# A hybrid decoder block on one core: k, the recurrent gate and both merge gates as seven products of half blocks

## What is computed

```
h = rms_norm(x, norm_mix_g)
proj = h @ w_in                      # 1024 x 7168: xr, gr, q, k, v, g0, g1, 1024 columns each
gates = sigmoid(g0, g1)
y_rnn = rglru_branch(xr, gr, ...)    # conv, gates r and i, linear recurrence, times gelu(gr)
y_att = diff_attention(q, k, v, ...) # 8 heads
merged = gates[0] * (y_rnn @ w_proj_rnn) + gates[1] * (y_att @ w_proj_att)
x = x + merged @ w_out
x = x + moe_ffn(rms_norm(x, norm_ffn_g), ...)   # top 4 of 32 experts
return rms_norm(x, norm_final_g)
```

## Time and profile before

| | |
|---|---|
| median of 3 executions | 1226.13 us (1225.16 to 1226.57) |
| profiled execution | 1225.36 us, of which the span from first to last instruction is 1223.6 |
| TensorE busy | 1165.2 us, 95% |
| VectorE, ScalarE, GpSimd busy | 294.6, 177.3 and 41.3 us |
| mean granted TensorE clock | 0.992 |
| transfers | 452.86 MB, mean 370 GB/s |

### The profile page before, as it was taken

How to read it: one execution, slowest core, us unless ns; L and a number is a source line. 1 busy time by engine, 2 the same in 40 slices (tenths; PEclk the granted TensorE clock), 3 DMA queues, 4 the chain that set the end, 5 groups by cost and what they waited for, 6 DMA issues and landing times.

```text
span 1223.6 us, 13719 instructions
## 1 busy us (share of the span) xinstructions
PE 1165.2 (95%) x5598; PEld 581.3 (48%) x5598; DVE 294.6 (24%) x611; ACT 177.3 (14%) x354; POOL 41.3 (3%) x35
## 2 busy tenths in 40 slices
PE   9999999999999999999999989898998989898997
PEld 7588888885533434333343424333333333342432
DVE  2915656222322120211212120202021111111112
ACT  2123433102310101101010101000010101010102
POOL 1000005600000000000000000000000000000000
PEclk9999999999999999999999999999999999999999
DMA  9555534775999999999999999999999999999996
GB/s 289 183 181 206 206 138 147 282 292 223 370 399 426 428 432 428 435 425 435 427 435 425 435 427 437 424 436 426 437 428 433 430 432 428 432 430 428 433 423 273
DMA packets 51114, 452.86 MB, mean 370 GB/s; under 512 B 7412, under 2 KB 8558, under 8 KB 32142
## 3 DMA queue, kind: packets, MB, share of 16 engines
q1 hardware_dynamic: 51086, 452.47, 89.3%
HBM read 450.35 MB, written 1.06 MB: 369 GB/s over the span
## 4 chain that ended last, share of the span: by engine, by line
PE 66%; DMA 31%; DVE 1%; SPq 1%; issue 0%; ACT 0%; DVEq 0%; ACTq 0%
PE bank L1648 25%; PE bank L1385 17%; DMA arena<-in_w_up_e 16%; PE banks L1648 9%; DMA arena<-in_w_gate_e 7%; DMA w_gate_sb<-in_w_gate_e 5%; PE banks L1597 3%; DMA w_down_sb<-in_w_down_e 3%; PE bank L1545 2%; PE bank L1402 1%; PE banks L1419 1%; PE bank L1419 1%; PE bank L1691 1%; PE banks L1787 1%; PE banks L1843 1%; PE bank L1843 1%
## 5 line engine op out<-in xcount | busy, mean ns | idle before, releaser
L1648 PE MATMUL bank<-arena 128*64 128x512 f32 x1032 | 238.7, 607 | 21.6 <-DMA arena<-in_w_gate_e 13.6
L1385 PE MATMUL bank<-arena,w_down_sb 128*128 128x256 f32 x960 | 210.0, 380 | 0.0
L1385 PEld LDWEIGHTS bank<-arena,w_down_sb 128*128 128x128 f32 x960 | 181.3, 190 | 26.8 <-issue 1.5
L1648 PEld LDWEIGHTS bank<-arena 128*64 128x64 f32 x1032 | 72.6, 139 | 162.5 <-issue 146.6
L1648 PE MATMUL bank<-w_gate_sb,arena 128*64 128x512 f32 x508 | 117.6, 610 | 9.7 <-DMA w_gate_sb<-in_w_gate_e 9.7
L1648 PE MATMUL bank<-w_up_sb,arena 128*64 128x512 f32 x508 | 112.4, 594 | 13.8 <-DMA w_up_sb<-in_w_up_e 13.8
L1648 PE MATMUL bank<-w_down_sb,arena 128*64 128x512 f32 x480 | 105.5, 592 | 0.0
L1260 DVE TENSOR_SCALAR arena<-bank 128x512 f32<-128x512 f32 x32 | 22.1, 692 | 256.5 <-PE bank L1648 255.2
L1648 PEld LDWEIGHTS bank<-w_up_sb,arena 128*64 128x64 f32 x508 | 35.5, 137 | 85.5 <-issue 64.9
L1648 PEld LDWEIGHTS bank<-w_gate_sb,arena 128*64 128x64 f32 x508 | 35.4, 140 | 81.3 <-issue 67.3
L1172 DVE TENSOR_TENSOR arena<-banks,g2T 128x512 f32<-128x512 f32 (+1 forms) x32 | 21.9, 684 | 200.5 <-PE banks L1597 199.7
(11 more groups left out here) (318 smaller groups left out, 832.4 us busy)
## 6 DMA issues: line engine op xcount, KB each, us to landing
w_down_sb<-in_w_down_e SPq DMA_DIRECT2D x30, 2048.0 KB, 34.5
arena<-in_w_up_e SPq DMA_DIRECT2D x13, 4096.0 KB, 39.5
w_up_sb<-in_w_up_e SPq DMA_DIRECT2D x13, 4096.0 KB, 37.6
arena<-in_w_gate_e SPq DMA_DIRECT2D x13, 4096.0 KB, 30.8
w_gate_sb<-in_w_gate_e SPq DMA_DIRECT2D x12, 4096.0 KB, 30.1
arena<-in_w_down_e SPq DMA_DIRECT2D x14, 2048.0 KB, 29.3
w_gate_sb<-in_w_down_e SPq DMA_DIRECT2D x14, 2048.0 KB, 29.3
w_down_sb<-in_w_in SPq DMA_DIRECT2D x12, 2048.0 KB, 8.2
```

The lines of the kernel that those rows point to most:

```text
L1385: ins = eng.matmul(ps[:, n * T:(n + 1) * T], w[:, k, (2 * b + n) * P:(2 * b + n + 1) * P], rhs[:, k, :], start=(k == 0), stop=(k == KC - 1))
L1648: ins = eng.matmul(ps[b * JB:(b + 1) * JB, :], lhsT, w[:, h * CH:(h + 1) * CH], **flags)
```

## The change

k, gr, g0 and g1 are no longer in the list of chunks. Each is made by seven block products (28 units in place of 16). The weights of one of them are loaded as four blocks of 512 x 512 (1 MB, `block_load`); VectorE makes two sums of weights (`block_sum_one`, `block_sum_two`), GpSimd two more from the second (128x2048 elements each); `block_product` is 16 matmuls with a 128x128 block of weights or sums as the loaded operand and 128 tokens or token sums moving, and takes the token sums that v made. ScalarE takes out the first product and the upper left quarter (products 0 and 2, which add up in one bank), VectorE adds the five other parts from PSUM (128x512 each) to what lies in SBUF (`block_part`). The tanh of the three other quarters of g0 and g1 follows in `block_tanh`. The heads' loop has 11 steps with two of these units each (one in the last). Exp and Tanh of the recurrence move in front of q's outputs, all eight scans in front of the heads' loop, between the parts of k; the sums of gr's weights too. The first two gelu instructions of VectorE move from step 5 to step 6. Four semaphores of loads and that of GpSimd's memset are used again.

```diff
+        WQ = [WG[:, 2 * n:2 * n + 2, :]... for n in range(4)]
+        DQ = [wst[:, n // 2, n % 2 * KQ:(n % 2 + 1) * KQ, :] for n in range(4)]
+        EQ = tile(8, KQ)
+        blocks_at = [(WQ[0], WQ[1], WQ[2], DQ[0]), (WQ[0], WQ[3], DQ[3], DQ[2]),
+                     (WQ[0], DQ[1], WQ[1], DQ[0]), (WQ[0], WQ[3], DQ[2], UQ)]
+        sums_at = [(WQ[1], EQ, UQ, DQ[1]), (WQ[3], WQ[2], EQ, UQ), (DQ[1], DQ[3], WQ[2], EQ), (WQ[3], WQ[1], DQ[3], WQ[2])]
+        block_tile = [kT, xrT, iT, rT]
...
 # SyncE
+            eng.wait_ge(s["unit_done"], unit("v", 7) + 1)
+            block_load(0, 0)
+            block_load(0, 1)
+            chunk(5)
+            block_load(0, 2)
+            block_load(1, 1)
...
+            eng.wait_ge(s["unit_done"], unit("q", 1) + 1)
+            block_load(0, 3)
+            eng.wait_ge(s["unit_done"], unit("q", 3) + 1)
+            block_load(1, 3)
+            block_load(1, 2)
+            eng.wait_ge(s["unit_done"], block_done(0, 0))
+            eng.wait_ge(s["job_tiles_then_sums_ready"], block_pool_sums(0, 1))
+            block_load(1, 0)
...
 # GpSimd
+            for j in range(len(BLOCKED)):
+                eng.wait_ge(s["sums_ready"], block_sums(j, 2))
+                eng.wait_ge(block_loaded[0], 16 * (j + 2))
+                if j > 0:
+                    eng.wait_ge(s["unit_done"], block_done(j - 1, 1))
+                    eng.wait_ge(s["job_tiles_then_sums_ready"], block_pool_sums(j - 1, 2))
+                eng.tensor_tensor(three, two, b11, ALU.subtract).then_inc(s["job_tiles_then_sums_ready"], 1)
+                eng.wait_ge(block_loaded[2], 16 * (j + 2))
+                if j > 0:
+                    eng.wait_ge(s["unit_done"], block_done(j - 1, 3))
+                eng.tensor_tensor(four, b21, two, ALU.subtract).then_inc(s["job_tiles_then_sums_ready"], 1)
 # VectorE
+            def block_part(j, n):
+                eng.wait_ge(s["unit_done"], block_done(j, n))
...
+                eng.tensor_tensor(out, part, quarters(bank[unit(BLOCKED[j], n) % 2]), ALU.add).then_inc(s["parts_ready"], 1)
+            block_sum_one(0)
             eng.wait_ge(s["decay_ready"], 2 * KC)
             link(eng.tensor_scalar(xcT[:, :, :], yrT[:, :, :], 1.0, None, ALU.add))
-            link(eng.reciprocal(xcT[:, :, :], xcT[:, :, :]))
+            link(eng.reciprocal(xcT[:, 0:KQ, :], xcT[:, 0:KQ, :]))
+            block_sum_two(0)
+            link(eng.reciprocal(xcT[:, KQ:KC, :], xcT[:, KQ:KC, :]))
...
+            block_part(0, 1)
             eng.wait_ge(s["multiplier_ready"], 1)
             link(eng.tensor_tensor(iT[:, :, :], iT[:, :, :], rT[:, :, :], ALU.mult))
+            block_sum_one(1)
+            block_sum_two(1)
+            for n in range(3, 7):
+                block_part(0, n)
+                for c in (2 * n - 6, 2 * n - 5):
+                    ins = eng.tensor_tensor_scan(yrT[:, c, :], xrT[:, c, :], iT[:, c, :], 0.0, ALU.mult, ALU.add)
...
+            for step in range(11):
                 if 1 <= step <= H:
                     weights_in(step - 1)
+                for n in (2 * step, 2 * step + 1):
+                    if n < 21:
+                        block_part(1 + n // 7, n % 7)
                 if step < H:
                     scores_in(step)
+                if step in (0, 4):
+                    block_sum_one(2 if step == 0 else 3)
+                if step in (1, 5):
+                    block_sum_two(2 if step == 1 else 3)
 # TensorE
+            def block_product(j, n):
...
+                if n < 2:
+                    if j == 0:
+                        eng.wait_ge(s["unit_out"], u - 1)
+                    else:
+                        eng.wait_ge(s["parts_ready"], block_parts(j - 1, n + 4))
+                elif n in (2, 4):
+                    eng.wait_ge(s["unit_out"], block_out(j, n // 2))
+                else:
+                    eng.wait_ge(s["parts_ready"], block_parts(j, {3: 1, 5: 2, 6: 3}[n]))
...
+                if n in (1, 4):
+                    eng.wait_ge(s["sums_ready"], block_sums(j, 2))
+                if n in (3, 5):
+                    eng.wait_ge(s["job_tiles_then_sums_ready"], block_pool_sums(j, n // 2))
...
+                for f in range(KQ):
+                    for k in range(KQ):
+                        ins = eng.matmul(ps[:, f * P:(f + 1) * P], w[:, k, f * P:(f + 1) * P], tokens[:, k, :],
+                                         start=(n in (0, 1, 3, 4) and f == 0 and k == 0), stop=(k == KQ - 1),
+                                         skip_group_check=True)
```

More of the change, by code:

```diff
@@ L422, in apart @@
                 eng.dma_start(place, src[:, k, :]).then_inc(done, 16)
[L424 to L446, removed]
@@ new lines, in _ @@
+            swap_halves(6, 8, s["conv_swapped_high"])
+            eng.wait_ge(s["unit_done"], unit("v", 7) + 1)
[4 more added lines that the diff above has]
+            block_load(1, 1)
+            eng.wait_ge(s["bias_rows_cleared"], 1)
+            for copy in range(3):
+                rows = slice(copy * NE, (copy + 1) * NE)
+                for m, name in enumerate(["b_gate_e", "b_up_e", "b_down_e"]):
+                    eng.dma_start(brow[rows, m, :], A[name][0]).then_inc(s["late_tables_loaded"], 16)
@@ new lines, in _ @@
+            apart(3, "w_up_e", 1, s["first_steps_loaded"])
+            eng.wait_ge(s["unit_done"], block_done(3, 3))
+            chunk(7)
+            eng.wait_ge(s["unit_done"], block_done(3, 5))
+            steps("w_gate_e", 0, KQ, KC - 1, 0, half_loaded[0][1])
+            steps("w_down_e", 0, KC - 1, KC, 0, s["steps_ahead_loaded"])
+            eng.wait_ge(s["unit_done"], block_done(3, 6))
+            out_chunk(1)
+            for i in range(7, len(STREAM)):
+                if i > 7:
+                    chunk(i)
@@ L698, in _ @@
                                ).then_inc(s["decay_ready"], 1)
-            unit_out(unit("k"))
+            unit_out(unit("q"))
             eng.wait_ge(s["bias_tile_loaded"], 32)
@@ L728, in head_out @@
                                ).then_inc(s["head_out"], 1)
[L730 to L733, removed]
+            for step in range(11):
+                for n in (2 * step, 2 * step + 1):
+                    if n % 7 == 0 and n < 21:
+                        block_one_out(1 + n // 7)
+                    if n % 7 == 2:
+                        block_first_quarter_out(1 + n // 7)
+                if step < H:
                     exps(step)
@@ L996, in scores_in @@
+            ins.then_inc(s["scan_ready"], 1)
             def scores_in(h):
@@ L1090, in _ @@
                                          ).then_inc(s["att_ready"], 1)
-            for u in range(unit("prnn", 3), unit("patt", 3) + 1):
+            gated(unit("prnn", 3))
+            eng.wait_ge(s["unit_out"], block_out(3, 2))
+            eng.wait_ge(s["tanh_ready"], 3)
+            for u in range(unit("patt"), unit("patt", 3) + 1):
                 gated(u)
@@ L1499, in head @@
                            ).then_inc(s["head_done"], 1)
-            for step in range(12):
-                product(unit("gr") + step, rhs=hT)
+            for step in range(11):
+                for n in (2 * step, 2 * step + 1):
+                    if n < 21:
+                        block_product(1 + n // 7, n % 7)
                 if step < H:
```

240 lines of the change are left out of this document (174 added, 66 removed).

## The result

The changed kernel takes **1249.5 us** (median of four executions, 1248.07 to 1250.33) against 1226.35 of the kernel before in the same comparison: a ratio of 1.019, interval 1.0177 to 1.0203, 23.2 us slower. I had said 1240, with a range up to 1248. The direction and the places are as told, the size isn't: +23.2 where the sum said +14.7. The profiled execution has a span of 1247.4 us, 23.8 more than before, and a mean clock of 0.981.

What follows compares the result with a forecast made beforehand. TensorE was taken to bound the kernel until the expert stage, shifts passing on one to one. -10.2 + 4.5 + 13.5 + 3.9 + 3.0 = +14.7; 1225.36 + 14.7 + 0.8 = 1240.9, said 1240; range 1215 to 1248, likeliest 1230 to 1248.

Steps and rivals of the forecast that it cites:

- TensorE's units: k, gr, g0, g1: 16 units of 6.91 us become 28 of 3.58, a gain of 10.2 us (other end 14.7).
- A: Between k and gr: GpSimd's sums hold VectorE's second scan, so k's last product waits 4.5 us (0 to 7.9).
- B: Steps 2 and 5 of the heads: GpSimd's sums hold the weights twice; waits 6.9, 6.2 and 0.4 behind, 13.5 us.
- C: End of the recurrent branch: w_proj_rnn waits for L1045 and L1048, slowed by GpSimd's bias-row work, 3.9 us (1.4 to 5.5).
- clock: TensorE at half clock after two waits longer than 6 us, 1.5 us lost each: 3.0 us (0 to 6).
- Weight loads stop hiding: Rival: in the 28 units each record adds 0.108 us to its load, +97 us, 1314 us in all; chance 0.02.
- The turns: VectorE and GpSimd alternate by whole instructions, so each pair of GpSimd sums holds VectorE instructions with SBUF inputs twice.
- my doubling: GpSimd's sum of 2048 columns taken as twice the 2.11 us of one of 1024: 4.22 us (3.8 to 5.1).
- They pass beside: Rival: GpSimd's sums run beside VectorE's work without holding it; 1217 us, 1213 to 1219, chance 0.21.
- the walk: Following the engine queues with these durations from k to the recurrent end, sums holding twice; 1240 us, chance 0.66.

Runs made afterwards that it cites:

- experiment 1: Kernel before plus four unused GpSimd subtractions of 128x2048, two released when head 1 is exponentiated, two at head 5: 1240.46 us, +15.5, ratio 1.0133.
- experiment 10: Changed kernel with each GpSimd sum cut into four instructions of 128x512: 1229.53 us, ratio 1.0029; into eight of 128x256: 1226.34 us, ratio 1.0004.
- experiment 5: Changed kernel with GpSimd's two sums for gr waiting until VectorE's eight scans are done: 1240.83 us, +15.4 against the kernel before, ratio 1.0123.
- experiment 2: Changed kernel with GpSimd's sums for g0 and g1 waiting for the attention weights of heads 1, 2, 5 and 6: 1234.0 us, +9.1 against the kernel before.
- experiment 8: Changed kernel with bias rows behind g0's last block, GpSimd's sums behind scans and head weights, last gelu instructions in step 8: 1215.94 us, ratio 0.9923 to kernel before.
- experiment 4: Changed kernel with the nine bias-row loads issued behind the last block of g0, some 130 us: 1244.44 us, +19.0 against the kernel before, ratio 1.0153.
- experiment 3: Changed kernel with the nine bias-row loads issued behind gr's blocks instead of ahead of k's fourth block: 1250.27 us, +25.4 against the kernel before, ratio 1.0205.
- Experiment 7: Changed kernel with 24 unused identity matmuls in each of TensorE's waits for the weights of heads 1 and 5: 1243.91 us, +19.0 against the kernel before.

## Why the prediction was right or wrong

| term | said | trace of after | what went wrong |
|---|---|---|---|
| TensorE's units | -10.2 | -10.5 | right, 3.57 us for 3.58 |
| A, k to gr | +4.5 (0 to 7.9) | +9.8 | a load was late; the hold alone is 5.6 |
| B, heads | +13.5 | +12.3 | right, in part by luck |
| C, recurrent end | +3.9 | +2.4 | two instructions 1.3 us longer in all, not 2.5 |
| clock | +3.0 (0 to 6) | +7.8 | twice as long, and four of them |
| sum | +14.7 | +21.8 | |

**The units.** The step of the gather's weight loads held when carried over from six loads to 28 x 32. The Trainium skill (TensorE: Matmul & The Clock Gate, What overlaps and what doesn't) would let such loads overlap only in another row group; these don't change it, and a record takes 3.57 / 32 = 0.112 us with its load, so they hide all the same. "Weight loads stop hiding" falls.

**The turns.** Two holds a pair, a whole instruction each, as told (experiments 1 and 10). That a scan is held, which no row of before showed, is now shown (9.47 for 1.26, experiment 5); the Trainium skill's rule on two SBUF inputs (SBUF — State Buffer, Who interferes with whom) agrees with it. A sum on GpSimd takes 4.49 to 4.54 us where VectorE doesn't hold it in turn, not the 4.22 of my doubling. The Trainium skill's 4497 ns (GPSIMD Engine Reference, Performance versus the Vector engine) agrees with the trace.

That B comes out near is in part luck. Longer sums should have made the weights later than the 8.5 us that I told; but the own time of the two held instructions (0.58 us) passes inside the holds, which I hadn't taken off, and the weights are 8.45 us late in both steps (L1190 ends at 162.4, and would at 153.95). TensorE asks for them 2.0 and 2.7 us after they would be ready, where I had 1.6 and 2.3, and the 0.4 us in the step behind doesn't come. "They pass beside" was right in one respect: the same sums cost nothing where VectorE reads PSUM, reduces or waits (experiments 2 and 8). I had put the gaps of VectorE at 1.5 us in a step; what counts are the instructions that can be held, and between a head's weights and the next there is room for one sum.

**A failed at one step**: "the load for its second sum of k ... lands around 87.5". That is 7.1 us from its issue at 80.4, for which the prediction names no row (the 8.2 us of a chunk would give 88.6). It was issued at 80.26 and landed at 92.5, 12.25 us later. The change moves the nine loads of bias rows right in front of it (issued at 71.8 to 76.9 us; before, at 63.4 to 68.1), and I had passed over them. Everything behind it is then 5 us later: the sums of gr end at 115.1, not 109.6, the part at 125.2, not 120.2. By the walk, A's 9.8 us are the 4.5 of the hold that I had told and 5.3 of lateness; measured, the hold alone is 5.6 (experiment 4: my 4.5, with a load and two sums of GpSimd somewhat longer) and the late transfer alone 3.1 (experiment 5), and together they are 1.1 more than their sum. That the rows are the cause is shown by experiments 3 and 4: moved, k's block is there by 85.9; moved onto gr's block, that one is late.

**The clock was mis-sized**, and beyond my bound. I had one row, 3.4 us at half speed after 2.9 us of idle, 1.5 us lost, and gave it to two waits. After waits of 6 us the stretches are 6.8 us long and cost 1.7 to 2.2 each, and A and C brought one too. Experiment 7 shows that this part is real and is the clock's: the weights come as late as before, and the time falls.

**C** was over-sized. L1214 met a GpSimd sum that had only 0.7 us to go, and L1217 a cast that needs only 1.03 us undisturbed, so they took 2.87 and 3.02 us in place of 2.29, and not a turn of 2.1 us more.

**The range** ended at 1248 because I didn't add the ends of A and of the clock in full. Both were passed (9.8 against 7.9, 7.8 against 6), and together: a longer wait also brings the longer stretch.

## What to carry to other kernels

An idle GpSimd isn't free help: each of its instructions on SBUF can hold one VectorE instruction for its whole length, so a chain of short ones on the critical path pays first. Put such work behind the chain, or cut it in pieces, or see if VectorE has the gap itself; here the same 28 units gave +23 us with the sums ahead of the chain, and -9.5 with them behind it, the bias rows later and the last gelu instructions earlier. And when a load decides something, read what is issued in front of it.

## What was not expected of the hardware

Nine loads of 128 KB each (32 rows of 4 KB) weigh more in the queue than their bytes. The transfers moved 389 GB/s from 65 to 80 us of the changed kernel, and 242 from 80 to 90, when these loads and the block were under way, with the DMA engines as full (the last two numbers of a window are DMA share and GB/s):

```profile
65.00:80.00 15.00, 15.00 (x88) 12.81 (x81) 6.49 (x4) 12.91 (x31) 1.21 (x1) 1.00 1.05 389
80.00:90.00 10.00, 10.00 (x49) 8.79 (x48) 5.87 (x1) 1.19 (x2) 0.00 (x0) 1.00 1.01 242
```

Each of the nine took about 10.7 us to land. In experiment 4, where they are issued from 131 us on, it is the same: 225 GB/s from 135 to 140, at a share of 1.03. What in them is slow isn't shown.

GpSimd's one small memset takes 1.21 us in the changed kernel and 0.14 before. In both it starts just behind a TENSOR_SCALAR of VectorE over 2048 columns (1.23 us), 0.08 us behind it in the one and 0.02 in the other. In the changed kernel it ends with that instruction, as if held by it; why it isn't before, isn't shown. And a GpSimd sum whose two inputs are the same tensor took 3.6 us where two different ones take 4.5.
